# A fourth weight buffer, an earlier mixer split and an uneven dealing of gate products in a two-layer decoder kernel

## The reference, cut to what matters

```
u = x * (1 + scale1) + shift1
x = LayerNorm(alpha * x + (1 + gate1) * Mixer(u))
u = x * (1 + scale2) + shift2
x = LayerNorm(alpha * x + (1 + gate2) * (silu(u @ Wa) * (u @ Wb)) @ Wout)
Mixer(u): y_nsa = nsa_attention(...) @ w_bn;  y_diff = diff_attention(...) @ w_bd
          (sigmoid(g_a) * y_nsa + sigmoid(g_b) * y_diff) @ w_o,  g = u @ w_in[:, gates]
```

## Time and profile before

| | us |
|---|---|
| median of 3 runs | 1686.99 |
| lowest, highest | 1684.29, 1687.72 |
| the profiled execution's own time | 1685.16 |
| its span | 1683.3 |
| TensorE busy | 1623.5 |
| VectorE (DVE) busy | 1001.8 |
| ScalarE (ACT) busy | 623.5 |
| mean granted TensorE clock | 0.991 of full |

### The profile page before, as it was taken

One profiled execution on the slowest core, in us unless ns is written; L12 is line 12 of the kernel. 1 busy time (PEld: TensorE's weight loads), 2 busy tenths in 40 slices (PEclk: granted clock), 3 DMA queues, 4 the chain that ended last, 5 costly groups with the idle time before them and its releaser, 6 DMA issues.

```text
span 1683.3 us, 21326 instructions
## 1 busy us (share of the span) xinstructions
PE 1623.5 (96%) x8406; PEld 1277.1 (76%) x8406; DVE 1001.8 (60%) x1557; ACT 623.5 (37%) x1117; POOL 51.7 (3%) x102
## 2 busy tenths in 40 slices
PE   6999999999999999999989999999999999999997
PEld 3778677677778888888868776766777788888886
DVE  2777687758685555546567657766557533333444
ACT  3432454445253322222253325445534533222221
POOL 1000000000001001100000000000000000000000
PEclk8999999999999999999999999999999999999999
DMA  9754222134327666664427231111222233333332
GB/s 304 219 168 128 74 63 64 51 99 140 101 64 211 187 194 183 188 185 148 140 53 200 75 88 38 39 38 34 80 88 88 84 92 100 101 100 119 91 93 74
DMA packets 278450, 193.07 MB, mean 115 GB/s; under 512 B 8344, under 2 KB 264912, under 8 KB 278352
## 3 DMA queue, kind: packets, MB, share of 16 engines
q1 hardware_dynamic: 264112, 147.95, 30.4%
q0 software_dynamic: 12320, 43.11, 8.6%
q10 hardware_dynamic: 1920, 0.66, 0.2%
HBM read 189.59 MB, written 2.10 MB: 114 GB/s over the span
## 4 chain that ended last, share of the span: by engine, by line
PE 87%; DVE 7%; ACT 2%; issue 2%; DMA 1%; SPq 0%; DVEq 0%; ACTq 0%
PE banks L1587 22%; PE banks L1589 22%; PE banks L1588 22%; PE banks L1709 3%; PE banks L1740 3%; PE banks L1768 2%; DMA ada_first<-in_w_ada_dram 1%; PE banks L1629 1%; PE banks L1715 1%; PE banks L1625 1%; PE banks L1626 1%; DVE w_lo L957 1%; PE banks L1719 1%; PE banks L1644 1%; PE banks L1645 1%
## 5 line engine op out<-in xcount | busy, mean ns | idle before, releaser
L1587 PE MATMUL banks<-u_hi,w_hi 128*128 128x512 f32 x1144 | 470.5, 411 | 15.8 <-DVE w_lo L957 12.5
L957 DVE TENSOR_TENSOR w_lo<-ring,w_hi 128x1024 fp32r<-128x1024 f32 (+2 forms) x243 | 290.6, 1198 | 298.9 <-ACT w_hi L696 298.0
L1589 PE MATMUL banks<-u_hi,w_lo 128*128 128x512 f32 x1144 | 449.5, 393 | 0.0
L1588 PE MATMUL banks<-u_lo,w_hi 128*128 128x512 f32 x1144 | 449.0, 392 | 0.0
L696 ACT ACTIVATE w_hi<-ring 128x1024 fp32r<-128x1024 f32 (+2 forms) x246 | 253.8, 1032 | 198.5 <-PE banks L1589 74.5
L1587 PEld LDWEIGHTS banks<-u_hi,w_hi 128*128 128x128 f32 x1144 | 216.5, 189 | 67.9 <-DVE w_lo L957 13.2
L1589 PEld LDWEIGHTS banks<-u_hi,w_lo 128*128 128x128 f32 x1144 | 216.2, 189 | 46.5
L1588 PEld LDWEIGHTS banks<-u_lo,w_hi 128*128 128x128 f32 x1144 | 217.2, 190 | 35.8
L849 ACT ACTIVATE probs<-banks,neg_max 128x128 f32<-128x128 f32 (+3 forms) x192 | 99.2, 525 | 159.5 <-DVE neg_max L1376 159.5
L1587 PE MATMUL banks<-h_hi,w_hi 128*128 128x512 f32 x352 | 138.5, 394 | 0.0
L1589 PE MATMUL banks<-h_hi,w_lo 128*128 128x512 f32 x352 | 137.0, 389 | 0.0
(11 more groups left out here) (253 smaller groups left out, 2145.4 us busy)
## 6 DMA issues: line engine op xcount, KB each, us to landing
ring<-in_w_ffn_in_dram SPq DMA_DIRECT2D x88, 512.0 KB, 3.9
ada_ring<-in_w_ada_dram POOLq DMA_DIRECT2D x80, 512.0 KB, 4.3
ring<-in_w_in_dram SPq DMA_DIRECT2D x72, 512.0 KB, 3.8
ring<-in_w_ffn_out_dram SPq DMA_DIRECT2D x32, 448.0 KB, 3.4
ada_first<-in_w_ada_dram SPq DMA_DIRECT2D x16, 512.0 KB, 8.5
ring<-in_w_out_dram SPq DMA_DIRECT2D x16, 512.0 KB, 3.6
ring<-in_w_ffn_out_dram SPq DMA_DIRECT2D x16, 512.0 KB, 4.1
w<-in_cmp_w_k_dram SPq DMA_DIRECT2D x8, 512.0 KB, 5.6
```

The lines of the kernel that those rows point to most:

```text
L957: V.tensor_tensor(lo, src, hi.bitcast(fp32), ALU.subtract).then_inc(split_lo, 1)
L1587: M(bank, wh[:, block], sh[:, k, :], start=start, stop=False)
L1588: M(bank, wh[:, block], sl[:, k, :], start=False, stop=False)
L1589: return M(bank, wl[:, block], sh[:, k, :], start=False, stop=stop)
```

## The change

It has five edits. (1) fb1 in both layers and kwn in layer 1 (`FOURTH_SPLIT`) get a buffer of their own, on the arena's blocks 40 to 43, and are prepared at the end of the layer norm, without a wait for a weight slot. (2) mix_hi and mix_lo move to blocks 20 to 35, merged_* to 46 to 61; ACT's wait for gm15 before the split goes, and DVE does the first two low parts after its second transposed tile. The squares of the first norm and the source of `keep_busy` move with them. (3) In the last block of `project_first` each job's three matmuls stand together, so that the first job is done first; the wait for the low input comes before the first job's third matmul. (4) The one-element Silu moves ahead of the sub-layer's inputs. (5) `gate_units` deals two products to each step and one or two more at listed steps; two of the last step's four are issued in the step after it, ahead of the last turn.

```diff
+def is_fourth(l, name):
+    return name == FOURTH_SPLIT[0] or (name == FOURTH_SPLIT[1] and l > 0)
+FOURTH_SPLIT = ("fb1", "kwn")
@@ prepared_at
-            if nl < DEPTH and SPLIT[ni] not in FIRST_SPLIT and ...
+            if nl < DEPTH and SPLIT[ni] not in FIRST_SPLIT + FOURTH_SPLIT and ...
@@
+MORE_UNITS = {1: 2, 3: 1, 6: 1, 8: 2, 10: 1, 13: 1, 15: 1, 20: 1, 24: 1, 28: 1, 32: 1, 36: 1, STEPS - 1: 2}
+UNIT_AT = [0]
+for _t in range(STEPS):
+    UNIT_AT.append(UNIT_AT[-1] + 2 + MORE_UNITS.get(_t, 0))
 def gate_units(t):
-    n = GM_IN * KD
-    return [divmod(u, KD) for u in range(n * t // STEPS, n * (t + 1) // STEPS)]
+    return [divmod(u, KD) for u in range(UNIT_AT[t], UNIT_AT[t + 1])]
@@ arena
+        fourth_hi = at("fourth_hi", 40, 2, fp32r)...
+        fourth_lo = at("fourth_lo", 42, 2, fp32r)...
-        merged_hi = at("merged_hi", 20, KD, fp32r)
-        merged_lo = at("merged_lo", 28, KD, fp32r)
+        merged_hi = at("merged_hi", 46, KD, fp32r)
+        merged_lo = at("merged_lo", 46 + KD, KD, fp32r)
-        mix_hi = at("mix_hi", 46, KD, fp32r)
-        mix_lo = at("mix_lo", 46 + KD, KD, fp32r)
+        mix_hi = at("mix_hi", 20, KD, fp32r)
+        mix_lo = at("mix_lo", 20 + KD, KD, fp32r)
-        squares = at("squares", 46, KD)
+        squares_of = at("squares0", 20, KD), at("squares1", 46, KD)
@@ split_slot
+            if is_fourth(l, name):
+                return fourth_hi[:, 0:size], fourth_lo[:, 0:size]
@@ prepare (ACT)
-                if n >= NQ:
+                if n >= NQ and not is_fourth(l, name):
@@ layernorm (ACT): after std_ready; after the inputs
+                if which == 0:
+                    nc.scalar.activation(table_out[:, :], eps[:, :], ACT.Silu)
...
-                if which == 0:
-                    nc.scalar.activation(table_out[:, :], eps[:, :], ACT.Silu)
+                if not last:
+                    prepare(l + which, FOURTH_SPLIT[which])
@@ gates 12 to 15 (ACT), m == 15
-                        wait_done(act, l, "gm15")
@@ transposed tiles of q_raw (DVE)
+                    if i == 1:
+                        mix_low(l, 0)
+                        mix_low(l, 1)
+                for k in range(2, KD):
+                    mix_low(l, k)
@@ project_first
+                    if k == KD - 1:
+                        for j, (name, bank) in enumerate(zip(names, out)):
+                            wh, wl = split_slot(l, name)
+                            M(bank, wh[:, block], sh[:, k, :], start=False, stop=False)
+                            M(bank, wl[:, block], sh[:, k, :], start=False, stop=False)
+                            if j == 0:
+                                pe.wait_ge(ready, count + k + 1)
+                            done(l, name, M(bank, wh[:, block], sl[:, k, :], start=False, stop=True))
+                        break
@@ keep_busy
-                    src = merged_hi if which == 0 else h_hi
+                    src = mix_lo if which == 0 else h_hi
@@ attention steps (TensorE)
-                    units = gate_units(t) if t < STEPS else []
-                    for m, k in units[:1]:
+                    units = gate_units(min(t, STEPS - 1))
+                    units = units[2:] if t == STEPS else units[:2] if t == STEPS - 1 else units if t < STEPS else []
+                    for m, k in units if t == STEPS else units[:1]:
                         merge_gate(l, m, k)
                     if 1 <= t <= STEPS:
                         turn(l, t - 1)
-                    for m, k in units[1:]:
+                    for m, k in () if t == STEPS else units[1:]:
                         merge_gate(l, m, k)
```

More of the change, by code:

```diff
@@ L137, in prepared_at @@
             nl, ni = divmod(l * len(SPLIT) + i + NQ - 1, len(SPLIT))
-            if nl < DEPTH and SPLIT[ni] not in FIRST_SPLIT and (nl, SPLIT[ni]) not in FIRST_LAYER_SPLIT:
+            if nl < DEPTH and SPLIT[ni] not in FIRST_SPLIT + FOURTH_SPLIT and (nl, SPLIT[ni]) not in FIRST_LAYER_SPLIT:
                 out.append((nl, SPLIT[ni]))
@@ L165 @@
 BY_DVE = [sum(kind != "diff" for _, _, kind, _ in SEQUENCE[:t + 1]) for t in range(STEPS)]
+MORE_UNITS = {1: 2, 3: 1, 6: 1, 8: 2, 10: 1, 13: 1, 15: 1, 20: 1, 24: 1, 28: 1, 32: 1, 36: 1, STEPS - 1: 2}
+UNIT_AT = [0]
+for _t in range(STEPS):
+    UNIT_AT.append(UNIT_AT[-1] + 2 + MORE_UNITS.get(_t, 0))
+assert UNIT_AT[-1] == GM_IN * KD
 def gate_units(t):
-    n = GM_IN * KD
-    return [divmod(u, KD) for u in range(n * t // STEPS, n * (t + 1) // STEPS)]
+    return [divmod(u, KD) for u in range(UNIT_AT[t], UNIT_AT[t + 1])]
 ADA_GROUPS = [(0, j) for j in range(2, 6)] + [(l, j) for l in range(1, DEPTH) for j in range(6)]
@@ L254, in build @@
         v_all = at("v_tok", 44, 2)
+        fourth_hi = at("fourth_hi", 40, 2, fp32r)[:, :, :].rearrange("p a n -> p (a n)")
+        fourth_lo = at("fourth_lo", 42, 2, fp32r)[:, :, :].rearrange("p a n -> p (a n)")
         kc2_all = at("kc2", 0, 4)
@@ L261, in build @@
         hid_tok = at("hid_tok", 11, 1)[:, 0, 0:CMP_HIDDEN]
-        merged_hi = at("merged_hi", 20, KD, fp32r)
-        merged_lo = at("merged_lo", 28, KD, fp32r)
-        merged_raw = at("merged_raw", 28, KD)
+        merged_hi = at("merged_hi", 46, KD, fp32r)
+        merged_lo = at("merged_lo", 46 + KD, KD, fp32r)
+        merged_raw = at("merged_raw", 46 + KD, KD)
         h_hi = at("h_hi", 0, KF, fp32r)
@@ L751, in layernorm @@
                 n = 2 * l + which
+                squares = squares_of[which]
                 last = l == DEPTH - 1 and which == 1
@@ L1208, in _, with mix_low @@
             V.memset(t1[:, 0:1], 0.0).then_inc(lam_summed, 1)
+            def mix_low(l, k):
+                dve.wait_ge(mix_high, l * KD + k + 1)
+                src = q_rot[:, k, :] if k < 4 else q_raw[:, k - 4, :]
+                V.tensor_tensor(mix_lo[:, k, :], src, mix_hi[:, k, :].bitcast(fp32), ALU.subtract)\
+                    .then_inc(mix_ready, 1)
             def merged_low(l, m):
@@ L1628, in project_first @@
                     for name, bank in zip(names, out):
-                        last = M(bank, split_slot(l, name)[0][:, block], sl[:, k, :], start=False, stop=k == KD - 1)
-                        if k == KD - 1:
-                            done(l, name, last)
+                        M(bank, split_slot(l, name)[0][:, block], sl[:, k, :], start=False, stop=False)
             def tokens(l, jobs, width):
```

## The result

The changed kernel takes 1665.95 us in the median of 4 runs (1665.68 to 1667.36), the kernel before 1685.64 on the same chip (1681.88 to 1687.72). The ratio is 0.9887, 95% interval 0.9867 to 0.9907. The forecast was 1668.0, range 1660 to 1676. It started from a median before of 1686.99; that median is 1.35 lower here, which is most of the 2.05 between forecast and measurement. The profiled execution took 1667.36 with a span of 1665.5, against a span of 1683.3 before: 17.8 less. On the profile's page TensorE does the same 8406 matmuls.

The account below looks back on a forecast made before the run. TensorE, busy 1623.5 of 1683.3 us, was the bound, so only its waits and low clock could give: 5.1 + 1.5 + 4.8 + 3.1 + 0.9 + 0 + 3.9 = 19.3 off 1685.2, plus 1.8 for the median, said as 1668; range 1660 to 1676.

Parts of the forecast that it names:

- fb1: Own buffer for fb1: the 2.57 us wait goes in each layer, 5.1, plus 1.5 of low clock in layer 0.
- mixer's split: Split before gm15 ends: TensorE's wait of 1.54 for the first mix_lo goes in each layer, 3.1 us; bounds 1.5 and 3.9.
- gate products: Uneven dealing in attention: idle time falls from 10.1 to 6.2 despite new collisions, a gain of 3.9 us; bounds -1 and 9.
- kwn: Own buffer, layer 1: the 5.22 wait goes, DVE's chain moves 4.8 earlier, new vsg waits; gain 4.8 us, bounds 3.5 and 7.9.
- rival 3: Low clock returns behind vsg0's new waits or in fb1's product, and a late bank costs 0.5 per fb1: 1671 to 1673; 0.08.
- wo0 earlier: wo0 done two matmuls sooner, shortening wo2's 0.71 wait for its bank by 0.45 per layer: 0.9 us, bounds 0 and 1.4.
- Table load: The moved Silu table load is hidden by DVE's centring and TensorE's spread in the norm: cost nothing, bounds 0 and 0.3.
- the first: Rival: in attention, gate dealing brings nothing or loses; total gain 15.4 us or less, 1672 to 1675; chance 0.18.
- The second: Rival: waits go in full, 7.9 at kwn for 4.8, up to 9 in attention for 3.9: 1660 to 1664; chance 0.12.
- The fourth: Rival: the table switch costs more than its load, each feed-forward part starting 1.1 us later: 1670; chance 0.03.
- The fifth: Rival: slower, TensorE falling to its 1.2 GHz level in the attention steps: 1688 to 1698; chance 0.02.
- The sixth: Rival: fb1 and kwn wait for their ring load or a bank instead, attention as before: 1681 to 1687; chance 0.05.

Follow-up runs that it names:

- e5: The changed kernel with the one-element Silu back behind the sub-layer's inputs, ahead of fb1's high part; 1667.19 us in one execution.
- e2: The changed kernel with fb1 back in the three rotating slots, kwn still in its own buffer; 1670.53 us, 0.9920 of the kernel before.
- e1: The changed kernel with the 96 gate products dealt evenly again; 1667.13 us, 0.9898 of the kernel before.
- e3: The changed kernel with the old order in the last block of the first products, all jobs finishing together; 1667.01 us in one execution.
- e12: The kernel of e7 run again beside the changed kernel on one chip; 1662.33 us, 0.9862 of the kernel before.
- e4: The changed kernel with ACT's wait for gm15 put back before the mixer's split, DVE keeping its new order; 1670.98 us, 0.9926 of the kernel before.
- e6: The changed kernel with square_diff one step later, in the sixth step of a tile; 1665.01 us in one execution.
- e7: The changed kernel with the 16 extra gate products dealt clear of save_diff, square_diff and layer 0's adaLN rows; 1662.31 us, 0.9861 of the kernel before.
- e13: e10 with the rope of ksl ahead of qn0's low part (vsg0, vsg1, vsg2, rope, qn0, rope, qn1); 1658.04 us, 0.9847 of the kernel before.
- e8: The changed kernel with layer 1's DVE order turned: vsg0's low part behind vc's copy, vsg1's and vsg2's each before a rope; 1665.59 us, 0.9880.
- after: The changed kernel itself, as every follow-up edit starts from it; 1665.95 us, 0.9887 of the kernel before.
- e10: The changed kernel with e7's dealing and e8's order, both ropes of ksl and kwn behind qn0's low part; 1661.60 us, 0.9858 of the kernel before.

## Why the prediction was right

The forecast's mechanism held: each named wait went, and where another was named in its place it came, but for vsg1's. That the sum behind the start-up was 19.05 for 19.3 is partly luck. Three terms were off, fb1 by +0.7, the mixer's split by +1.0 and the gate products by -2.0, and they cancelled.

- **fb1**: 7.3 (4.46 + 2.84) for 5.1 + 1.5. The step was right; a wait costs about 0.3 more than its bracket. In layer 1, where the clock was whole before and after, a wait of 2.57 gave 2.84 back; in e5 a wait of 1.11 cost 1.4, in e2 1.65 cost 1.9. Two parts of that can be read from rows. Matmuls of 512 columns start 0.23 apart and take 0.39 (496.96 and 497.19), so without a wait 0.16 of each lies under the one before it, and a bracket counts only from that one's end. And the first matmul behind the wait takes 0.50 instead of 0.39. Together that is 0.27: 2.57 + 0.27 = 2.84. One working was off: fa0 is done six matmuls before the end of the block, but only four sooner than before. The time that was worked out with it, 497.6, counts from the end and so holds.
- **kwn**: 4.85 (6.30 less 1.45) for 4.8. The step that made it right was to follow DVE's chain behind the wait instead of taking the wait and its low clock for 7.9. The wait for vsg0 was forecast at 1.7 and is 1.83. Three waits were named; two came, and the sign "all stretches but the start at a clock of 1.00" failed. In this profile the clock fell behind the first wait and vsg1's wait isn't there. In e1, e2, e3, e5 and e12 the clock didn't fall and vsg1's wait of 1.0 is there. The stage takes 36.7 in all of them: the chain on DVE sets its end, and a slower TensorE only waits less. So rival 3's low clock did come, and it cost nothing.
- **Mixer's split**: 4.1 (1.68 + 0.33 + 1.70 + 0.38) for 3.1, above my 3.9. The bracket of 1.54 gave 1.7 in each layer, by the 0.16 explained at fb1. The step that failed was to stop at yn0: the stage behind it, up to wo0, got shorter too, by 0.33 and 0.38. Most of that is the wait in front of yn1 for DVE to read yn0's bank. It went from 0.55 to 0.30 in layer 0 (shown above) and from 0.59 to 0.31 in layer 1. The rest is yn0's first matmul, which no longer stands behind a wait and takes 0.39 instead of 0.47. e4 shows that this second stage hangs on the same chain (1.38 and 1.34 longer).
- **wo0 earlier**: 0.9 for 0.9, and e3 confirms it.
- **Table load**: nothing for nothing, the norm's stage is 6.16 before and after; e5 gives its price where it isn't hidden, 1.4 a layer.
- **Gate products**: 1.9 for 3.9, the term that was off most. The collisions that I named were right in place and size, and e6 shows the cause of the first. What failed is the size of the idle time after, 4.0 and 2.2 in the sum: it is 4.7 and 3.0, 1.5 us more. The sum allowed 0.4 per layer for short waits, and they come to 1.2, with the new waits of TensorE for its own last values among them. The other 0.5 is busy time, which the sum took as fixed: over the two attention stages it grew by 0.35 and 0.19. Which instructions make that up wasn't isolated.
- **Rivals**: the first (dealing brings nothing) is out by e1, but not far. The second was right that more was there: e7 and e13 get 3.6 in attention and 4.3 behind kwn, though neither lay in this change. The fourth is out by e5 and the 6.16 above. The fifth is out, the clock in attention is 1.00. The sixth is out too: fb1 and kwn start without a wait.

## What to carry over

When a wait is removed, follow the queue of the engine that was waited for to its next late item, and count the gain from how far that item moves. A chain without a gap on another engine keeps its end when it is only reordered: e8 gave nothing. Moving work behind what the next reader needs gains only if the engine doesn't then stand idle for something else. With both ropes behind qn0 it stood idle for a transfer and nothing was gained; with one rope in that gap and one behind it, 4.3 us were. When filler work is dealt to the waits of one engine, look at which steps of the other engines the deal moves work into.

## What I had not expected of the hardware

- A long wait didn't always bring the low clock. Behind a wait of 1.83 us (after), 2.46 (e10) and 2.68 (e8) the mean granted clock of the next 6 us was 0.72; behind 1.79 and 1.78 at the same place (e12, e2) and behind 1.65 (e2) it was 1.00. The same 2.57 did both in the kernel before. Even one kernel did both. e7, behind a wait of 1.83, and e12, the same kernel behind 1.79, show in the 6 us from vsg0's start:

```profile
873.72:879.72 6.00, 6.00 (x35) 6.00 (x36) 5.79 (x11) 0.67 (x1) 0.00 (x0) 0.72 0.48 137
...
873.60:879.60 6.00, 5.00 (x37) 4.78 (x37) 5.79 (x11) 0.67 (x1) 0.00 (x0) 1.00 0.49 137
```

  At the low clock TensorE is busy for all 6 us, at the full clock for 5.0, and both reach the hidden layer after 36.7 us. What decides between the two levels stays open.
- TensorE's small waits of 0.15 us for its own last results appear when a step's slack is gone, seven in a layer for three. So a wait that is filled doesn't bring all of its idle time.
